# Second feed-forward matrix by Strassen's scheme, in turn with 128-feature tiles of the first matrix

## The chip, the core and the metric

The kernel runs on one core of one Trainium2 chip. A core has a matrix engine (TensorE, PE in the profile), three engines that work element by element on 128 partitions (VectorE or DVE, ScalarE or ACT, GpSimd or POOL), and SyncE (SP), which here issues the large transfers from HBM. SBUF holds the operands; PSUM, eight banks of 128 x 512 numbers, takes the products. The metric is the device time of one execution in microseconds (us), lower is better. The kernel before takes 2152.32 us (median of three runs, 2152.02 to 2153.08).

## The reference

Two hybrid attention layers run over 256 positions of 2048 features; then comes a block with block-sparse attention, a convolution and a feed-forward. Only that last part is touched:

```python
f = rms_norm(h, g_ffn_pre)                                   # 256 x 2048
f = jnp.square(jax.nn.relu(f @ w_ff1)) @ w_ff2               # 2048 -> 8192 -> 2048
h = h + rms_norm(f, g_ffn_post)
```

All data is float32. The result must be near that of float32 products.

## The kernel before

**How a float32 product is made.** The operands of PE are in fp32r, a format that keeps fewer bits. So every operand is split in two: `high`, the number rounded to fp32r, and `low`, what is left, rounded too. A product is the sum of three: high by high, high by low and low by high. Weights stream from HBM in blocks of 512 KB (128 partitions x 1024 numbers): SP loads a block into `raw` (a ring of four), ACT copies it to `high` with rounding (`round_block`, L934), DVE subtracts `high` from `raw` and writes `low` (`low_part`, L490), and PE multiplies. For 61 blocks of an earlier stage POOL makes `low` in DVE's stead, since DVE works there on the convolution (L1682, L1726, L1718).

**The feed-forward.** 256 blocks, four quarters of 64. In a quarter, eight chunks of the first matrix come first (four blocks each, 256 hidden features each). These are computed with the features on the partitions: a weight tile is the stationary operand, high and low of the normed input (`xhl`) stream past it, 512 columns at once (L682), and `low` of the weights meets the high half of the input, 256 columns (L699). A block has eight matmuls of 512 and eight of 256 columns. Then ACT and DVE add the cross term, take the square of the positive part and split it into high and low (`relu_square` L1242 to L1246, L1300, L1820). Four chunks of the second matrix follow (eight blocks each): here the hidden tile is the stationary operand and 512 columns of weights stream past it. A block holds two tiles of 128 hidden features by 512 outputs; with two halves of the positions and three partial products that makes 12 matmuls of 512 columns (L686, L687, L702). At a chunk's end DVE adds two banks of PSUM to the running sum (`ff_sum`, L1635).

**What sets the order.** All of it is written out by hand; each engine goes through its own list and waits on semaphores. `slots` interleaves a block's work with side work; PE goes through `weight_block` in the order of the plan.

Of the kernel before, what the change touches and what calls it, by code (L numbers as in the profile page):

```python
# [39 lines left out]
P = 128  # L40
S = 256
# [13 lines left out]
NQ = 4  # L55
# [39 lines left out]
def plan(a):  # L95
# [77 lines left out]
    for q in range(NQ):  # L173
        f1 = [("f1", q, j) for j in range(8)]
        if q == 0:

            run(*[chunk(k, a["w_ff1_2"][0], D * q + 256 * j, width=256, flipped=True) for j, k in enumerate(f1[:2])])
        for j, k in enumerate(f1):
            if q or j >= 2:
                flip(k, a["w_ff1_2"][0], D * q + 256 * j)  # L180
        for n, (col, width) in enumerate(FCOLS):
            add(("f2", q, n), a["w_ff2_2"][0], col, width=width, row0=D * q)
# [6 lines left out]
FF0, FF_SLOTS = BLOCK2 + BLOCK2_SLOTS, 64  # L189
# [13 lines left out]
F2_LAST = [NQ * FF_SLOTS - 8 * n + 1 for n in (3, 2, 1)]  # L203
# [26 lines left out]
def build(nc, a, out):  # L230
    by, chunk_at, acc_users = plan(a)
    with ExitStack() as ctx:
# [3 lines left out]
        def sem(name):  # L236
            return ctx.enter_context(nc.semaphore(name))

# [84 lines left out]
        rowp, rowf = cut(work, 4096, D), cut(work, 10480, D)  # L323
# [21 lines left out]
        def vec(name, n):  # L345
# [9 lines left out]
        rstd2, rstdm, rstd3, rstd4, sq3, nmr = (vec(k, 2) for k in ("rstd2", "rstdm", "rstd3", "rstd4", "sq3", "nmr"))  # L355
# [13 lines left out]
            relu_ready fsq_ready fin_ready out_done dve_done norm_dve rows_half mw_landed mw_high mw_low mw_ready csum_ready""".split()  # L369
# [7 lines left out]
         fsq_ready, fin_ready, out_done, dve_done, norm_dve, rows_half, mw_landed, mw_high, mw_low, mw_ready, csum_ready) = (sem(n) for n in names)  # L377
# [72 lines left out]
        def sums(kind, *at):  # L450

            return {"o": 0, "oa": 2 * NC, "ob": 2 * NC + 4, "f2": 3 * NC + 4}[kind] + (NF if kind == "f2" else NC) * sum(at[:-1]) + at[-1] + 1
# [35 lines left out]
        def low_part(eng, g, ready):  # L488
            eng.wait_ge(high_ready, g + 1)
            eng.tensor_tensor(part(low, g), part(raw, g), part(high, g).bitcast(F32), ALU.subtract).then_inc(ready, 1)  # L490
# [5 lines left out]
        def _(pe):  # L496
# [113 lines left out]
            def operands_ready(c, i):  # L610
# [15 lines left out]
                elif k[0] in ("o", "oa", "ob", "f2") and k[-1]:  # L626
# [7 lines left out]
                elif k[0] == "ob" and i == 0:  # L634
                    pe.wait_ge(yt_ready, 32 + H2)
                elif k[0] == "ob":
                    pe.wait_ge(ct_ready, i)
                elif k[0] == "f2":
                    pe.wait_ge(yt_ready, 40 + 8 * k[1] + i + 1)

            def weight_block(g, rows=(0, 1), between=None):
# [6 lines left out]
                vhs, vls, both = (yh, yl, yhl) if k[0] in ("mk", "mv", "o", "oa", "ob", "f2") else (xh, xl, None)  # L648
# [5 lines left out]
                tiles = [(t, c.kt0 + c.nk * i + t, s) for t in range(c.nk) for s in rows[:len(outs)]]  # L654
# [12 lines left out]
                def with_high(start, stop):  # L667
                    pe.wait_ge(high_ready, g + 1)
                    for t, kt, s in tiles:
                        if k in (("f1", 0, 0), ("f1", 0, 1)) and (t, s) == (2, rows[0]):  # L670
# [51 lines left out]
                else:  # L722
# [3 lines left out]
                    ins = with_low(g == c.blocks[-1])  # L726
                if 1 in rows:
                    ins.then_inc(block_used, 1)
                elif g == c.blocks[-1]:
# [185 lines left out]
            for b in range(NQ * FF_SLOTS):  # L915
# [4 lines left out]
                if b < NQ * FF_SLOTS - 4:  # L920
                    weight_block(FF0 + b)
            for s in range(ST):
                for b in range(NQ * FF_SLOTS - 4, NQ * FF_SLOTS):
                    weight_block(FF0 + b, (s,))
# [3 lines left out]
        def _(act):  # L928
# [18 lines left out]
            def cross_out(name):  # L947
# [4 lines left out]
                if flips.index(c):  # L952
                    act.wait_ge(folded, n)
                act.activation(cross, crosses(c), ACT.Copy).then_inc(cross_ready, 1)  # L954
# [74 lines left out]
            def squares(src, c, rows=(0, 1)):  # L1029
# [203 lines left out]
            def relu_square(name):  # L1233

                c = by[name]
# [738 lines left out]
```

## Time and profile before

| | |
|---|---|
| median of three runs | 2152.32 us |
| profiled execution: its own time (span) | 2150.6 us |
| PE busy | 2125.1 us (99%) |
| DVE busy | 1361.9 us (63%) |
| ACT busy | 1106.1 us (51%) |
| POOL busy | 156.2 us (7%) |
| DMA | 395.17 MB, mean 184 GB/s |

The profile is of one execution. Its span counts from the first to the last instruction. "Busy" of PE counts the modelled ends of its matmuls, which overlap, so that the mean duration of a matmul is longer than the distance from one to the next. The clock granted to PE is 1.00 (of 2.4 GHz) in all slices but the last few microseconds. In the two-engine view of a stretch the columns are: stretch, its length, then busy us and instruction count of PE, of its weight loads, of DVE, ACT and POOL, then PE's granted clock, the mean busy share of the 16 DMA engines and GB/s.

### The profile page before, as it was taken

To read this page: it belongs to the slowest core of one execution; us is meant where nothing else is said; L and a number is where in the kernel's file an instruction comes from. 1 tells how busy PE (TensorE), PEld (TensorE's weight loads), DVE (VectorE), ACT (ScalarE), POOL (GpSimd) and SP (SyncE) were. 2 spreads that over 40 slices of the span, in tenths; PEclk is the share of its full clock that TensorE was granted. 3 is DMA by queue.
4 is the path that set the end of the run, shared out by engine and by line. 5 is a ranking of instruction groups with operands and counts; after the bars stand their busy time and mean duration, and the time that the engine had idled before them with its cause. 6 is when DMAs were issued, how large, how long until landed. Compare 5 with 4: busy or idle time off the path is not lost. (4 is left out here: it accounts for less than half of the span.)

```text
span 2150.6 us, 29240 instructions
## 1 busy us (share of the span) xinstructions
PE 2125.1 (99%) x11602; PEld 1841.8 (86%) x11602; DVE 1361.9 (63%) x1979; ACT 1106.1 (51%) x1541; POOL 156.2 (7%) x78
## 2 busy tenths in 40 slices
PE   8999999999999999999999999999999999999998
PEld 7888888888988888888888888888888888888886
DVE  5554568875577558876578678766555555555555
ACT  4444554454464555555455455656435534544543
POOL 0000000000000000000007873000000000000000
PEclk9999999999999999999999999999999999999999
DMA  8666545655576655655656654646666666666664
GB/s 278 196 189 187 165 138 174 179 172 186 185 214 186 178 148 159 174 167 176 191 180 198 193 178 151 215 136 206 193 193 190 189 193 193 189 194 190 192 190 145
DMA packets 325031, 395.17 MB, mean 184 GB/s; under 512 B 20848, under 2 KB 252912, under 8 KB 324128
## 3 DMA queue, kind: packets, MB, share of 16 engines
q1 hardware_dynamic: 323104, 383.21, 59.0%
q0 software_dynamic: 1792, 10.10, 1.2%
q8 instruction: 92, 1.51, 0.3%
q14 instruction: 43, 0.35, 0.1%
HBM read 391.16 MB, written 2.10 MB: 183 GB/s over the span
## 5 line engine op out<-in xcount | busy, mean ns | idle before, releaser
L490 DVE TENSOR_TENSOR low<-raw,high 128x1024 fp32r<-128x1024 f32 (+2 forms) x672 | 809.9, 1209 | 639.0 <-ACT high L934 635.3
L934 ACT ACTIVATE high<-raw 128x1024 fp32r<-128x1024 f32 (+2 forms) x732 | 763.0, 1046 | 775.8 <-PE acc L682 201.7
L682 PE MATMUL acc<-xhl,high 128*128 128x512 f32 x3198 | 766.4, 391 | 0.0
L682 PEld LDWEIGHTS acc<-xhl,high 128*128 128x128 f32 x3198 | 587.0, 188 | 113.8 <-issue 0.7
L699 PE MATMUL acc<-xhl,low 128*128 128x256 f32 x3200 | 436.9, 286 | 1.9 <-DVE xhl L1792 1.4
L699 PEld LDWEIGHTS acc<-xhl,low 128*128 128x128 f32 x3200 | 414.4, 191 | 18.1 <-DVE xhl L1792 1.8
L686 PE MATMUL acc<-high,yhl 128*128 128x512 f32 (+1 forms) x1036 | 380.1, 373 | 2.2 <-DVE work L1718 1.6
L687 PE MATMUL acc<-high,yhl 128*128 128x512 f32 (+1 forms) x1036 | 378.8, 372 | 0.0
L702 PE MATMUL acc<-low,yhl 128*128 128x512 f32 (+1 forms) x1036 | 241.9, 374 | 0.2
L686 PEld LDWEIGHTS acc<-high,yhl 128*128 128x128 f32 x1036 | 195.2, 188 | 36.8 <-DVE work L1718 2.0
L687 PEld LDWEIGHTS acc<-high,yhl 128*128 128x128 f32 x1036 | 195.2, 188 | 33.8
L702 PEld LDWEIGHTS acc<-low,yhl 128*128 128x128 f32 x1036 | 182.9, 189 | 33.7 <-DVE yhl L1401 1.0
L490 POOL TENSOR_TENSOR low<-raw,high 128x1024 fp32r<-128x1024 f32 x61 | 147.9, 2437 | 81.2 <-ACT high L934 80.9
L1300 DVE TENSOR_TENSOR acc<-acc,cross 128x512 f32<-128x512 f32 x103 | 71.5, 694 | 37.2 <-ACT cross L954 37.0
L1682 DVE SCALAR_TENSOR_TENSOR tb<-work,params,tb 128x256 f32<-128x256 f32 x232 | 93.7, 480 | 0.0
L966 ACT ACTIVATE sc<-sc,small 128x128 f32<-128x128 f32 x64 | 28.6, 448 | 93.0 <-DVE small L1376 92.9
L686 PE MATMUL acc<-high,xhl 128*128 128x512 f32 (+2 forms) x224 | 73.7, 341 | 0.1
L687 PE MATMUL acc<-high,xhl 128*128 128x512 f32 (+2 forms) x224 | 73.1, 339 | 0.0
L702 PE MATMUL acc<-low,xhl 128*128 128x512 f32 (+2 forms) x320 | 72.7, 360 | 0.0
L954 ACT ACTIVATE cross<-acc 128x512 f32<-128x512 f32 x104 | 60.4, 581 | 1.9 <-PE acc L682 1.9
L702 PEld LDWEIGHTS acc<-low,xhl 128*128 128x128 f32 x320 | 53.7, 188 | 8.5 <-issue 1.3
L686 PEld LDWEIGHTS acc<-high,xhl 128*128 128x128 f32 x224 | 42.3, 189 | 5.2 <-issue 0.7
(228 smaller groups left out, 1286.9 us busy)
## 6 DMA issues: line engine op xcount, KB each, us to landing
raw<-in_w_in SPq DMA_DIRECT2D x328, 512.0 KB, 3.7
raw<-in_w_ff SPq DMA_DIRECT2D x256, 512.0 KB, 3.9
raw<-in_w_out SPq DMA_DIRECT2D x91, 512.0 KB, 4.3
raw<-in_w_mem_kv SPq DMA_DIRECT2D x32, 512.0 KB, 5.0
raw<-in_w_in SPq DMA_DIRECT2D x16, 256.0 KB, 2.7
raw<-in_w_out SPq DMA_DIRECT2D x10, 256.0 KB, 2.8
x_nat<-in_mem SPq DMA_DIRECT2D x4, 512.0 KB, 7.8
x_nat<-in_x POOLq DMA_DIRECT2D x4, 512.0 KB, 6.4
```

What stands on the lines that cost most here:

```text
L490: eng.tensor_tensor(part(low, g), part(raw, g), part(high, g).bitcast(F32), ALU.subtract).then_inc(ready, 1)
L682: ins = pe.matmul(acc[:, 2 * (c.acc % 2) + s, :], wh[:, t, at], vhl, start=first, stop=last)
L686: pe.matmul(outs[s], vh[:, at], wh[:, t, :], start=first, stop=False)
L687: ins = pe.matmul(outs[s], vl[:, at], wh[:, t, :], start=False, stop=last)
L699: ins = pe.matmul(acc[:, 2 * (c.acc % 2) + s, S:2 * S], wl[:, t, at], vh, start=crossed and t == 0, stop=last)
L702: ins = pe.matmul(outs[s], vh[:, at], wl[:, t, :], start=False, stop=last)
L934: act.activation(part(high, g), part(raw, g), ACT.Copy).then_inc(high_ready, 1)
L954: act.activation(cross, crosses(c), ACT.Copy).then_inc(cross_ready, 1)
L966: ins = act.activation(sc[:, j % 2, s, 0:n], src, ACT.Exp, bias=nmx[:, r:r + 1], accum_out=rs[:, r:r + 1])
L1300: dve.tensor_tensor(out, accs(c), cross, ALU.add).then_inc(folded, 1)
L1682: ins = dve.scalar_tensor_tensor(out=cv[:, ct, :] if tap == TAPS - 1 else sums_at, in0=src, scalar=w, in1=sums_at, op0=ALU.mult, op1=ALU.add)
```

## The change

The hidden layer has 64 tiles of 128 features. Tiles are taken in pairs; a pair by one half (1024) of the output columns is a 2 x 2 by 2 x 2 product of blocks: two position halves by two tiles, and two tiles by two column blocks of 512. Done plainly it takes eight block products. The change does 60 of the 64 such groups with seven block products (Winograd's form of Strassen's scheme), and the last four, half of the columns of pairs 28 to 31, plainly, as eight blocks (`last_block`).

- **PE** does the first 12 blocks of the first matrix as before. Then it goes in turn: `group(g)`, 21 matmuls of 512 columns (seven products, 14 with high weights, then seven with low), and `hidden_tile(g + 6)`, two blocks of one 128-feature tile of the first matrix, 16 matmuls of 512 and 16 of 256 columns. Seven banks of PSUM hold the products of four groups.
- **SP** loads a group as two transfers of 512 KB (`load_group`, into one of two buffers `bset`, when PE has finished the group two before), and the first matrix in blocks of eight row tiles by 128 columns.
- **POOL** makes, for each group, the four sums of weight blocks (`group_sums`: 512, 512 and 1024 columns), for each pair the four sums of hidden blocks (`pair_sums`: 128 columns each), and for every fourth group adds products to the running sums (`add_sums`: two of 1024).
- **ACT** rounds the seven weight blocks of a group (`split_h`: 1024, 1024, 1536 columns), the two blocks of the first matrix, the hidden tile out of PSUM (`tile_copy`) and the seven hidden blocks of a pair (`pair_h`, 896).
- **DVE** makes the low parts of all of these (`split_l`, `low_part`, `pair_l`), the squares (`hidden_rows`), and for every fourth group adds seven products out of PSUM (`sums_out`). `split_l` waits until POOL has made all sums of that group, since it writes over the weights.

The core of the diff, in the order plan, PE (`group` and its loop), DVE (`hidden_rows`, `split_l` and the loop), POOL (`group_sums` and the loop), SP:

```diff
-    for q in range(NQ):
-        f1 = [("f1", q, j) for j in range(8)]
...
-        for n, (col, width) in enumerate(FCOLS):
-            add(("f2", q, n), a["w_ff2_2"][0], col, width=width, row0=D * q)
+    for n in range(TILES_AHEAD, TILES):
+        add(("g1", n), w, P * n, width=P, nk=8)
+    for n in range(2, NF):
+        add(("f2", n), a["w_ff2_2"][0], CW * n, row0=P * (TILES - 8), kts=8)
...
+            def group(g):
...
+                pe.wait_ge(pair_ready, pair + 1)
+                hid, units = hidden(pair), bset_r[:, g % 2]
+                for n, (p, unit, combo_no) in enumerate(PRODUCTS):
+                    pe.wait_ge(split_high, 3 * g + (1, 1, 2, 2, 3, 3, 3)[n])
+                    if first:
+                        product_released(g // 4, p)
+                    for hl in range(2):
+                        pe.matmul(bank_of[p], hid[:, hl, combo_no, :], units[:, 7 + unit, :], start=first and hl == 0,
+                                  stop=False)
+                for n, (p, unit, combo_no) in enumerate(PRODUCTS):
+                    pe.wait_ge(split_low, 3 * g + (1, 1, 2, 2, 3, 3, 3)[n])
+                    ins = pe.matmul(bank_of[p], hid[:, 0, combo_no, :], units[:, unit, :], start=False, stop=last)
+                ins.then_inc(group_used, 1)
...
+            for g in range(GROUPS):
+                group(g)
+                if g + TILES_AHEAD < TILES:
+                    hidden_tile(g + TILES_AHEAD)
...
+            def hidden_rows(n):
...
+                dve.wait_ge(tile_out, n - TILES_AHEAD + 1)
+                link(dve.tensor_tensor(t[:, 0:S], t[:, 0:S], t[:, S:2 * S], ALU.add))
...
+                dve.scalar_tensor_tensor(out=combo[:, 1:3, :] if n % 2 else combo[:, 0:8:7, :], in0=v, scalar=0.0, in1=v,
+                                         op0=ALU.max, op1=ALU.mult).then_inc(relu_ready, 1)
...
+            def split_l(g, part_no):
+
+                dve.wait_ge(sum_step, 3 * g + 3)
+                dve.wait_ge(split_high, 3 * g + part_no + 1)
+                at, end = ((2, 4), (0, 2), (4, 7))[part_no]
+                dve.tensor_tensor(bset_r[:, g % 2, at:end, :], bset[:, g % 2, at:end, :], bset_r[:, g % 2, 7 + at:7 + end, :].bitcast(F32),
+                                  ALU.subtract).then_inc(split_low, 1)
...
+            for g in range(GROUPS):
+                n, ahead = g + TILES_AHEAD - 1, g + 1 < GROUPS
+                if g and n < TILES:
+                    hidden_rows(n)
+                if g:
+                    low_block(FF1 + 2 * g)
+                    low_block(FF1 + 2 * g + 1)
+                if ahead:
+                    split_l(g + 1, 0)
+                    split_l(g + 1, 1)
+                if g % 4 == 3:
+                    sums_out(g // 4)
+                if ahead:
+                    split_l(g + 1, 2)
+                if g % 2 == 0 and n < TILES:
+                    pair_l(g // 2 + 2)
...
+            def group_sums(g):
+
+                units = bset[:, g % 2]
+                pool.wait_ge(group_landed[g % 2][0], 16 * (g // 2 + 1))
+                pool.tensor_tensor(units[:, 1, :], units[:, 1, :], units[:, 0, :], ALU.subtract).then_inc(sum_step, 1)
...
+                pool.tensor_tensor(units[:, 4, :], units[:, 3, :], units[:, 1, :], ALU.subtract).then_inc(sum_step, 1)
+                pool.wait_ge(sum_step, 3 * g + 2)
+                t2 = units[:, 4, :].unsqueeze(1).broadcast_to([P, 2, CW])
+                pool.tensor_tensor(units[:, 5:7, :], t2, units[:, 0:3:2, :], ALU.subtract).then_inc(sum_step, 1)
...
+            for g in range(GROUPS):
+                if g + 1 < GROUPS:
+                    group_sums(g + 1)
+                if g % 2 == 0 and g + TILES_AHEAD - 1 < TILES:
+                    pair_sums(g // 2 + 2)
+                if g % 4 == 0 and g:
+                    add_sums(g // 4 - 1)
...
+            def load_group(g):
...
+                    sp.wait_ge(group_used, g - 1)
```

What this does to DVE's list, before: in the feed-forward, between two chunks of the first matrix. `low` and `raw` are the weight block, `yhl` the hidden rows, `acc` and `cross` are in PSUM and SBUF.

```order
L1300 TENSOR_TENSOR acc<-acc,cross 128x2x256
L490 TENSOR_TENSOR low<-raw,high 128x1024 x2
L1820 TENSOR_TENSOR yhl<-cb,yhl 128x512
L490 TENSOR_TENSOR low<-raw,high 128x1024 x2
L1300 TENSOR_TENSOR acc<-acc,cross 128x2x256
```

In its place stands, on DVE, for an even step (`bset`, `bset_r` are the weight blocks of a group, `combo` and `hid` the hidden blocks of a pair, `raw_r` the low block):

```order
L2014 TENSOR_TENSOR tile_b<-tile_b 128x256
L2017 SCALAR_TENSOR_TENSOR combo<-tile_b 128x256
L518 TENSOR_TENSOR raw_r<-raw,high 128x1024 x2
L2034 TENSOR_TENSOR bset_r<-bset,bset_r 128x1024 x2
L2034 TENSOR_TENSOR bset_r<-bset,bset_r 128x1536
L2027 TENSOR_TENSOR hid<-combo,hid 128x896
```

and for every fourth step, with the products `sbank`, `tb` and `acc` in PSUM, the running sums `msum`, and `au` and `u` between them:

```order
L2014 TENSOR_TENSOR cross<-cross 128x256
L2017 SCALAR_TENSOR_TENSOR combo<-cross 128x2x128
L518 TENSOR_TENSOR raw_r<-raw,high 128x1024 x2
L2034 TENSOR_TENSOR bset_r<-bset,bset_r 128x1024 x2
L2051 TENSOR_TENSOR msum<-msum,sbank 128x512
L2052 TENSOR_TENSOR msum<-msum,tb 128x512
L2053 TENSOR_TENSOR msum<-msum,acc 128x512
L2055 TENSOR_TENSOR msum<-msum,acc 128x512
L2059 TENSOR_TENSOR au<-au,acc 128x512
L2061 TENSOR_TENSOR u<-au,acc 128x512
L2062 TENSOR_TENSOR msum<-msum,acc 128x512
L2034 TENSOR_TENSOR bset_r<-bset,bset_r 128x1536
```

A step on DVE is thus two low blocks of the first matrix and seven low blocks of 512 for the group, where before it was one instruction of 1024 columns for each 512 KB.

POOL's list before, to its end (`L490` are the 61 low blocks of the earlier stage; the two last transfers load gain vectors):

```order
L1907 DMA yf<-in_ln_gain 128x2048
L1908 DMA yf<-in_ln_bias 128x2048
L490 ISA
L490 TENSOR_TENSOR low<-raw,high 128x1024 x61
L1913 DMA work<-in_g_mix_post 128x2048
L1916 DMA work<-in_g_ffn_post 128x2048
L232 UNCONDITIONAL_BRANCH
```

POOL's list now, from the middle of the feed-forward; in all there are 60 such triples on `bset`, 32 such quadruples on `combo` and 15 pairs on `msum`:

```order
L2242 TENSOR_TENSOR combo<-combo 128x128
L2243 TENSOR_TENSOR combo<-combo 128x128
L2245 TENSOR_TENSOR combo<-combo 128x128
L2247 TENSOR_TENSOR combo<-combo 128x128
L2253 TENSOR_TENSOR msum<-msum,au 128x1024
L2256 TENSOR_TENSOR msum<-msum,u 128x1024
L2230 TENSOR_TENSOR bset<-bset 128x512
L2233 TENSOR_TENSOR bset<-bset 128x512
L2236 TENSOR_TENSOR bset<-bset 128x1024
```

What POOL had after its last low block was only the two transfers; now it has three instructions for each group, between DVE's own.

## Rows read from the trace of the kernel before

**Rows 1.** The page: span, then busy time of each engine.

```profile
span 2150.6 us, 29240 instructions
PE 2125.1 (99%) x11602; PEld 1841.8 (86%) x11602; DVE 1361.9 (63%) x1979; ACT 1106.1 (51%) x1541; POOL 156.2 (7%) x78
```

**Rows 2.** Stretches of the feed-forward and of the end, busy us and granted clock.

```profile
1610.00:2100.00 490.00, 490.00 (x2521) 420.70 (x2520) 261.34 (x248) 241.79 (x278) 0.00 (x0) 1.00 0.62 191
2145.00:2151.00 6.00, 0.00 (x0) 0.00 (x0) 2.71 (x4) 0.00 (x0) 0.00 (x0) 0.68 0.49 175
```

**Rows 3.** Groups by shape inside 1610:2100: busy us, mean ns, then idle before.

```profile
L490 DVE TENSOR_TENSOR low<-raw,high 128x1024 fp32r<-128x1024 f32 x179 | 219.4, 1226 | 230.2 <-ACT high L934 230.2
L934 ACT ACTIVATE high<-raw 128x1024 fp32r<-128x1024 f32 x178 | 188.7, 1060 | 246.9 <-PE acc L699 71.8 <-PE acc L702 67.0 <-PE acc L687 61.1
L954 ACT ACTIVATE cross<-acc 128x512 f32<-128x512 f32 x24 | 13.9, 579 | 0.0
L1635 DVE SCALAR_TENSOR_TENSOR work<-acc,small,work 128x512 f32<-128x512 f32 x20 | 14.0, 745 | 0.0
L1820 DVE TENSOR_TENSOR yhl<-cb,yhl 128x512 fp32r<-128x512 f32 x24 | 16.4, 685 | 0.0
```

**Rows 4.** Timeline of PE (start us, us): first-matrix blocks, then second-matrix blocks.

```profile
1491.09 3.82 PE L682 MATMUL acc<-xhl,high 128*128 128x512 f32 x16
1496.66 3.82 PE L682 MATMUL acc<-xhl,high 128*128 128x512 f32 x16
...
2105.42 1.98 PE L702 MATMUL acc<-low,yhl 128*128 128x512 f32 x8
2110.86 1.52 PE L702 MATMUL acc<-low,yhl 128*128 128x512 f32 x6
```

**Rows 5.** Timeline of PE where twelve feed-forward blocks are done.

```profile
1468.82 3.82 PE L682 MATMUL acc<-xhl,high 128*128 128x512 f32 x16
```

**Rows 6.** Timeline of POOL, four of its 61 instructions beside busy DVE.

```profile
1141.73 2.99 POOL L490 TENSOR_TENSOR low<-raw,high 128x1024 fp32r<-128x1024 f32 x1 [52.79 <-ACT high L934]
...
1147.49 2.40 POOL L490 TENSOR_TENSOR low<-raw,high 128x1024 fp32r<-128x1024 f32 x1
1149.85 2.60 POOL L490 TENSOR_TENSOR low<-raw,high 128x1024 fp32r<-128x1024 f32 x1
...
1315.62 2.40 POOL L490 TENSOR_TENSOR low<-raw,high 128x1024 fp32r<-128x1024 f32 x1 [2.83 <-ACT high L934]
```

**Rows 7.** Timeline of DVE over the same time.

```profile
1140.10 2.36 DVE L490 TENSOR_TENSOR low<-raw,high 128x1024 fp32r<-128x1024 f32 x2
...
1144.01 1.26 DVE L1718 TENSOR_TENSOR work<-work,cb 128x512 f32<-128x512 f32 x1
...
1148.22 1.95 DVE L1726 SCALAR_TENSOR_TENSOR work<-work,params,cb 128x256 f32<-128x256 f32 x1 [2.35 <-ACT cb L1192]
1150.10 2.64 DVE L1726 SCALAR_TENSOR_TENSOR work<-work,params,cb 128x256 f32<-128x256 f32 x1
...
1316.93 2.17 DVE L490 TENSOR_TENSOR low<-raw,high 128x1024 fp32r<-128x1024 f32 x1 [0.17 <-ACT high L934]
```

**Rows 8.** Groups by shape: POOL in 1240:1310, DVE in 1141:1316.

```profile
L490 POOL TENSOR_TENSOR low<-raw,high 128x1024 fp32r<-128x1024 f32 x23 | 54.8, 2399 | 15.0 <-ACT high L934 14.8
...
L1682 DVE SCALAR_TENSOR_TENSOR tb<-work,params,tb 128x256 f32<-128x256 f32 x217 | 87.4, 480 | 0.0
```

**Rows 9.** Timeline of PE, its last instruction.

```profile
2141.46 0.39 PE L687 MATMUL acc<-high,yhl 128*128 128x512 f32 x1
```

**Rows 10.** DMA issues in 1420:2110, KB each, median us to landing.

```profile
raw<-in_w_ff SPq DMA_DIRECT2D x249, 512.0 KB, 3.9
```

More of the change, by code:

```diff
@@ L653, in weight_block @@
                 wh, wl = part(high, g), part(low, g)
-                tiles = [(t, c.kt0 + c.nk * i + t, s) for t in range(c.nk) for s in rows[:len(outs)]]
+                tiles = [(t, c.kt0 + c.nk * i + t, s) for t in range(c.nk) for s in range(2)]
                 crossed = k == ("f1", 0, 0) and i == 0
@@ new lines, in product_released @@
+            def product_released(k, p):
+                if k == 0:
+                    if p in (5, 6, 7, 4):
+                        pe.wait_ge(relu_ready, 2 if p in (5, 6) else 3)
+                elif p == 1:
+                    pe.wait_ge(first_out, k)
+                else:
+                    pe.wait_ge(out_step, 7 * (k - 1) + OUT_STEP[p])
+            def group(g):
+                pair, _ = where(g)
+                first, last = pair % 4 == 0, pair % 4 == 3
+                pe.wait_ge(pair_ready, pair + 1)
[11 more added lines that the diff above has]
+                ins.then_inc(group_used, 1)
@@ new lines, in first_copy @@
+            def first_copy(k):
+                act.wait_ge(group_used, 4 * k + 4)
+                if k:
+                    act.wait_ge(out_added, 2 * k - 1)
+                act.activation(au[:, 0, :], bank_of[1], ACT.Copy).then_inc(first_out, 1)
+            cross_out(("f1", 0, 0))
+            round_block(FF0 + 10)
+            round_block(FF0 + 11)
+            cross_out(("f1", 0, 1))
+            pair_h(0)
+            round_block(FF1)
+            for part_no in range(3):
+                split_h(0, part_no)
@@ new lines, in _ @@
+            n_sq = 16 + 2 * NC
+            for g in range(BLOCKS - 4, BLOCKS - 1):
+                low_block(g)
+            dve.wait_ge(rowf_landed, 16)
+            gain_sums(0, n_sq + 2)
+            low_block(BLOCKS - 1)
+            gain_sums(1, n_sq + 4)
+            dve.wait_ge(block_used, by["f2", 2].blocks[-1] + 1)
+            for s in range(ST):
+                ins = dve.tensor_tensor(m_cols(2)[:, s, :], m_cols(2)[:, s, :], last_banks[2][s], ALU.add)
+            ins.then_inc(sum_ready, 1)
@@ L1834, in _ @@
+            dve.wait_ge(sum_ready, sums("f2", 2))
+            gain_sums(2, n_sq + 6)
+            for s in range(ST):
+                rows, at = m_cols(3)[:, s, :], slice(s, s + 1)
                 if s:
-                    acc_done(last)
+                    dve.wait_ge(block_used, BLOCKS)
                 else:
                     dve.wait_ge(rows_half, 1)
-                dve.scalar_tensor_tensor(out=rows, in0=accs(last)[:, s, :], scalar=sq3[:, at], in1=rows, op0=ALU.mult,
-                                         op1=ALU.add).then_inc(sum_ready, 1)
```

425 lines of the change are left out of this document (314 added, 111 removed).

## The prediction

> **What bounds the kernel now.** I read the page's busy times first. The reader is to see that PE is busy for 99% of a span of 2150.6 us, that DVE and ACT have 37 and 49% to spare, and that POOL is nearly idle [rows 1]. Then the stretch view of the middle of the feed-forward: PE is busy for all 490 of 490 us at the full clock, DVE for 261 us and ACT for 242 [rows 2]. The groups of that stretch say who waits for whom there: DVE sits idle before its low blocks until ACT has rounded, and ACT sits idle until PE frees a buffer [rows 3]. So PE alone sets the pace, and matmuls taken from it come off the end, as long as no other engine becomes slower than PE. The timelines give the pace. Two blocks of the first matrix take 1496.66 - 1491.09 = 5.57 us, 2.785 each, and two of the second 2110.86 - 2105.42 = 5.44 us, 2.72 each or 0.2267 us for each of its 12 matmuls of 512 columns [rows 4].
>
> **PE after the change.** The second matrix costs 128 x 2.72 = 348.2 us now. After, 60 groups of 21 matmuls are 60 x 4.76 = 285.6 us and eight plain blocks 21.8 us, together 307.4: 40.8 us less. The first matrix keeps its columns, 12 blocks and then 58 tiles of two blocks, 5.57 us each. One step (a group and a tile) is 10.33 us of PE. That is what the other engines must keep up with.
>
> **DVE and POOL by themselves.** DVE's instruction of 1024 columns takes 1.23 us, one of 512 takes 0.685 [rows 3]: 0.54 us for 512 columns and 0.14 fixed. Each step it has two low blocks (2.45), three splits of 1024, 1024 and 1536 (1.23 + 1.23 + 1.77 = 4.23), two of 256 columns for the squares (0.83), half of a pair's 896 columns (0.55), and a quarter of seven instructions of 512 out of PSUM, between 0.685 and 0.745 each [rows 3], 1.2. Sum 9.3 us: it fits in 10.33. POOL's instruction of 1024 columns takes 2.40 us where nothing disturbs it [rows 8]. Each step it has 2048 columns of group sums, half of 512 for a pair, a quarter of 2048 for the running sums: 2816 columns, 6.6 us. That fits too. ACT: 3584 columns of splits, two blocks, a tile, half a pair, by 1.06 us for 1024 and 0.58 for 512 [rows 3], is about 7.1 us. It fits.
>
> **DVE and POOL together.** They do not run beside each other. The only place where the trace shows both at once is the stretch in which POOL makes low blocks, and there the ends of the instructions tell it [rows 6, 7]:
> - POOL's block of 1315.62 ends at 1318.02. DVE's block, begun at 1316.93, ends at 1319.10, 1.08 us after POOL's end, though it takes 1.23 us alone: it did next to nothing while POOL ran.
> - POOL's block of 1141.73 ends at 1144.72; DVE's 512 columns of 1144.01 end 0.55 us later.
> - POOL's block of 1147.49 ends at 1149.89; DVE's 256 columns of 1148.22 end 0.28 us later. POOL's next ends at 1152.45; DVE's next ends again 0.29 us later, at 1152.74, after 2.64 us.
> - The other way round, POOL's block of 1141.73 begins while DVE's pair from 1140.10 runs to 1142.46, and takes 2.99 us in place of 2.40.
>
> All these DVE instructions read two operands in SBUF. L1682, which reads one in SBUF and one in PSUM, runs 217 times beside POOL at 480 ns [rows 8] and shows nothing of it. The Trainium skill (SBUF — State Buffer, section Who interferes with whom) says the same in general: a VectorE instruction with two SBUF inputs and a GpSimd instruction that reads SBUF share a port by an exclusive lock, and the second one blocks until the first is done. If it were a split of bandwidth instead, the block of 1316.93 would have got half of its columns done in the 1.09 us of overlap and ended near 1318.7; the trace has 1319.10.
>
> In the changed kernel nearly all of DVE's work (splits, low blocks, squares, pairs; all but the sums out of PSUM) reads twice from SBUF, and all of POOL's sums read SBUF. So their times add up. For a step:
> - DVE holds the port for 1.08 us for 1024 columns (above). 2048 + 3584 + 512 + 448 = 6592 columns: 6.95 us.
> - POOL holds it for the distance between two ends less DVE's part, 2.56 - 0.28 = 2.28 us for 1024 [rows 6, 7]. 2816 columns: 6.27 us.
> - The sums out of PSUM are 1.05 us in which DVE does nothing else; POOL could run beside them, but seldom has work just then. Changes of turn and short waits on DVE's own results: 0.1.
>
> The sum is 14.4 us for a step, against PE's 10.33. Its bounds: 13.2 if the sums out of PSUM lie wholly beside POOL, and 9.3 + 6.6 = 15.9 if whole durations add, fixed parts too. I take 14.4, since the rows show blocked instructions without their fixed part. For POOL's sums of 128 columns there is no row; by proportion 0.3 us each, with a fixed part like DVE's 0.44, which is 0.3 us a step at most and inside the bounds.
>
> Nothing else is later. The loop through the transfer: a group's buffer comes free at PE's end of a group, two transfers land 4 to 6 us later (3.9 us for one of 512 KB now, [rows 10]; the rows of the first matrix get half as long, which I put at up to 1 us), POOL's three sums with DVE's turns between them take 4.6 + 3.5, ACT has rounded meanwhile, DVE's three splits with POOL's turns 7, PE's last products 0.7. That is some 22 us for two steps of 28.8. On SP, what queues behind a `load_group` are the two blocks for two steps later.
>
> **The sum.** Twelve blocks are done at 1468.82 + 1.83 = 1470.6 us, half way through the 16 matmuls of that row [rows 5]. I add 5 us of waiting for the first group (POOL's first sums, ACT's and DVE's first splits in a line; 0 to 12), 4.8 for group 0, and 12 for the step in which DVE's list is shorter. Then 58 steps of 14.4 are 835.2. At the end 2 us for the release of the banks, 21.8 for the eight plain blocks, and from PE's last matmul to the end 2150.6 - 2141.85 = 8.8 us as now [rows 1, 9]. 1470.6 + 5 + 4.8 + 12 + 835.2 + 2 + 21.8 + 8.8 = 2360. The median of the runs is 1.7 us above the profiled span, so 2362 us. With 13.2 a step it is 70 less, 2292; with 15.9 it is 87 more, 2449.
>
> **Rivals.**
> - *The change works as counted: PE stays the bound.* DVE's and POOL's own sums, 9.3 and 6.6 us, are both below 10.33, so this is what busy times alone would say. 1470.6 + 5 + 4.8 + 59 x 4.76 + 58 x 5.57 + 21.8 + 8.8 = 2115, and 1.7: 2117 us, 1.6% faster. It needs POOL's plain f32 sums to leave DVE alone, where its f32 to fp32r low blocks do not. It decides at 10.33 us: DVE's 9.3 leave 1.0 us for all of POOL's 6.3. The five overlaps above speak against it. Chance 10%.
> - *The port is shared by turns, but POOL is faster at plain f32 than at its low blocks.* No row shows POOL with f32 output. If it were as fast as DVE, 1.23 us for 1024, its part would be 3.4 us, a step 11.4, the whole 2362 - 58 x 3.0 = 2188 us, still slower. Anything between lies between. Chance 9%.
> - *More than the sum.* PE waits some 4 us in each step. It has no such gap in the middle of the kernel now; after its last matmul the granted clock of 2145:2151 is 0.68, a mean of the full level and of half [rows 2]. If the clock fell to 1.2 GHz in each gap and a third of a step's matmuls ran at half speed, a step would cost PE 10.33 x 1.33 = 13.8 us, which still fits in 14.4. With half of them it is 15.5, 1.1 us more than the port's 14.4, and the whole 2362 + 58 x 1.1 = 2426 us; with all of them 20.7 us and over 2700. It decides at four tenths of the matmuls. The Trainium skill (TensorE: Matmul & The Clock Gate, section Why this matters for your kernels) warns of this fall after idle gaps; that the gap is long enough here, no row shows. Chance 7%.
>
> **Chances and range.** The forecast of adding up (2292 to 2449) has 74%. Faster by over 0.2% (which is about what a measurement of this kernel can tell from no change) comes only with the first rival: 10%. Within 0.2%: 1%, a step of 10.8 us by chance. Slower: 89%. The range 2240 to 2440 leaves out the first rival, the lower half of the second, and the top of the third and of the sum.
>
> **What would show it.** In the profile after: PE busy well under 99%, with some 70% in the stretch from 1500 us on, and its idle time ended by DVE's splits (L2034). POOL busy some 400 us more. The mean of DVE's 1024-column splits and low blocks at 1.8 to 2.5 us in place of 1.23, while its sums out of PSUM stay at 0.69. The distance between two groups on PE 14.4 us. I am wrong if the DVE durations stay at 1.23 beside POOL; then the end is near 2117. If PE's idle time is ended by DMA or by ACT, the loop through the transfer was the bound and my margin of 7 us there was wrong. If the granted clock falls in the stretch, the third rival is at work.

## The result, and the profile after

The changed kernel takes 2356.5 us (median of four, 2354.2 to 2357.8) against 2152.7 for the kernel before: a ratio of 1.0945, 95% interval 1.093 to 1.0961. Its profiled execution has a span of 2356.0 us. The forecast was 2362.

The page after, which answers to [rows 1]: span, busy times, and of the 40 slices those of PE, DVE, POOL and PE's clock.

```profile
span 2356.0 us, 29862 instructions
PE 2176.2 (92%) x11422; PEld 1856.9 (79%) x11422; DVE 1844.8 (78%) x2205; ACT 1170.1 (50%) x1584; POOL 839.1 (36%) x417
...
PE   8999999999999999999999999788888888888886
...
DVE  5555578665765687757867867899999999999996
...
POOL 0000000000000000000587202687878787878882
PEclk9999999999999999999999999898989898988898
```

The last 15 slices are the changed part. DVE goes from mostly 5 tenths to 9, POOL from 0 to 8, and PE, at 9 there before, falls to 8. The stretch view of its middle (columns as in [rows 2]) and the waits of PE there (who waited for whom, us in all, times, longest):

```profile
1600.00:2100.00 500.00, 421.23 (x1878) 344.16 (x1878) 498.48 (x329) 227.12 (x241) 400.69 (x195) 0.89 0.50 150
...
PE obank L804 <- DVE raw_r L518: 62.7, 30, 4.5
PE sbank L836 <- DVE hid L2027: 12.9, 5, 2.7
```

DVE is busy for 498 of 500 us and no longer waits for anyone; PE is busy for 421 at a mean clock of 0.89 and waits for DVE. In the groups by shape of that stretch, DVE and then POOL, the mean of one instruction is what to look at, beside [rows 3, 8]:

```profile
L2034 DVE TENSOR_TENSOR bset_r<-bset,bset_r 128x1024 fp32r<-128x1024 f32 x72 | 122.3, 1737 | 0.0
L518 DVE TENSOR_TENSOR raw_r<-raw,high 128x1024 fp32r<-128x1024 f32 x70 | 116.0, 1697 | 0.0
L2034 DVE TENSOR_TENSOR bset_r<-bset,bset_r 128x1536 fp32r<-128x1536 f32 x36 | 88.6, 2461 | 0.0
L2027 DVE TENSOR_TENSOR hid<-combo,hid 128x896 fp32r<-128x896 f32 x18 | 49.1, 2727 | 0.0
L2014 DVE TENSOR_TENSOR cross<-cross 128x256 f32<-128x256 f32 x18 | 37.1, 2059 | 0.0
...
L2061 DVE TENSOR_TENSOR u<-au,acc 128x512 f32<-128x512 f32 x9 | 6.2, 687 | 0.3
...
L2236 POOL TENSOR_TENSOR bset<-bset 128x1024 f32<-128x1024 f32 x35 | 104.5, 2987 | 2.7
L2230 POOL TENSOR_TENSOR bset<-bset 128x512 f32<-128x512 f32 x36 | 70.5, 1959 | 47.3 <-DMA bset<-in_w_ff 47.3
L2245 POOL TENSOR_TENSOR combo<-combo 128x128 f32<-128x128 f32 x18 | 25.9, 1439 | 0.0
```

A block of 1024 columns takes DVE 1.70 to 1.74 us, where it took 1.23; the 256 columns on `cross` take 2.06, five times the 0.42 that they take with nobody in the way; the sums out of PSUM keep their 0.69 us. POOL's 1024 columns take 2.99 us, where a block of 1024 took 2.40, and its 128 columns 1.44; waits for the other engine count in all of these. Both are longer beside each other, and DVE only where it reads twice from SBUF. The timelines of DVE and then POOL show the turns:

```profile
1810.89 2.29 DVE L2034 TENSOR_TENSOR bset_r<-bset,bset_r 128x1024 fp32r<-128x1024 f32 x1
1813.11 2.31 DVE L2034 TENSOR_TENSOR bset_r<-bset,bset_r 128x1024 fp32r<-128x1024 f32 x1
1815.34 0.68 DVE L2051 TENSOR_TENSOR msum<-msum,sbank 128x512 f32<-128x512 f32 x1
...
1819.64 1.75 DVE L2034 TENSOR_TENSOR bset_r<-bset,bset_r 128x1536 fp32r<-128x1536 f32 x1
...
1810.44 1.66 POOL L2230 TENSOR_TENSOR bset<-bset 128x512 f32<-128x512 f32 x1 [2.03 <-DMA bset<-in_w_ff]
1812.25 2.09 POOL L2233 TENSOR_TENSOR bset<-bset 128x512 f32<-128x512 f32 x1
1814.41 3.25 POOL L2236 TENSOR_TENSOR bset<-bset 128x1024 f32<-128x1024 f32 x1
```

POOL's first sum ends at 1812.10 and DVE's block at 1813.18, 1.08 us later. POOL's second ends at 1814.34 and DVE's second block at 1815.42, 1.08 us later again, as in [rows 6, 7]. POOL's third, of 1024 columns, begins at 1814.41 and takes 3.25 us: it waits for the rest of DVE's block and then runs beside the sums out of PSUM, which pay nothing for it. The split of 1819.64, with POOL idle, takes 1.75 us.

### The profile page after: what moved, and what is told of

Its sections match the earlier page's. It is cut to its first block and busy times, and to the rows that moved or that the text cites. A ratio compares the mean times of both kernels' runs of the same rounds, so it can differ in the third digit from the quotient of the medians.

```text
span 2356.0 us, 29862 instructions
## 1 busy us (share of the span) xinstructions
PE 2176.2 (92%) x11422; PEld 1856.9 (79%) x11422; DVE 1844.8 (78%) x2205; ACT 1170.1 (50%) x1584; POOL 839.1 (36%) x417
## 5 line engine op out<-in xcount | busy, mean ns | idle before, releaser
L518 DVE TENSOR_TENSOR low<-raw,high 128x1024 fp32r<-128x1024 f32 (+2 forms) x428 | 512.0, 1202 | 337.0 <-ACT high L1099 333.4
L740 PE MATMUL acc<-xhl,high 128*128 128x512 f32 x2270 | 544.6, 391 | 0.0
L740 PEld LDWEIGHTS acc<-xhl,high 128*128 128x128 f32 x2270 | 416.5, 188 | 80.8 <-issue 0.7
L2034 DVE TENSOR_TENSOR bset_r<-bset,bset_r 128x1024 fp32r<-128x1024 f32 x180 | 341.9, 1945 | 0.0
L1413 ACT ACTIVATE bset_r<-bset 128x1024 fp32r<-128x1024 f32 x180 | 210.1, 1194 | 138.1 <-POOL bset L2230 71.4
L797 PE MATMUL obank<-xhl,high 128*128 128x512 f32 x928 | 246.2, 410 | 0.0
L797 PEld LDWEIGHTS obank<-xhl,high 128*128 128x128 f32 x928 | 182.5, 202 | 36.7
L518 DVE TENSOR_TENSOR raw_r<-raw,high 128x1024 fp32r<-128x1024 f32 x124 | 201.8, 1665 | 7.4 <-ACT high L1099 7.4
L744 PE MATMUL acc<-high,yhl 128*128 128x512 f32 (+1 forms) x524 | 180.9, 358 | 2.2 <-DVE work L1913 1.6
L745 PE MATMUL acc<-high,yhl 128*128 128x512 f32 (+1 forms) x524 | 179.7, 356 | 0.0
L518 POOL TENSOR_TENSOR low<-raw,high 128x1024 fp32r<-128x1024 f32 x61 | 147.9, 2436 | 81.2 <-ACT high L1099 80.9
L2236 POOL TENSOR_TENSOR bset<-bset 128x1024 f32<-128x1024 f32 x60 | 174.3, 2906 | 4.7
L836 PE MATMUL acc<-bset_r,hid 128*128 128x512 f32 x480 | 131.0, 414 | 12.1 <-DVE combo L2007 11.7
```

The source lines that it names most:

```text
L518: eng.tensor_tensor(out, part(raw, g), part(high, g).bitcast(F32), ALU.subtract).then_inc(ready, 1)
L740: ins = pe.matmul(acc[:, 2 * (c.acc % 2) + s, :], wh[:, t, at], vhl, start=first, stop=last)
L744: pe.matmul(outs[s], vh[:, at], wh[:, t, :], start=first, stop=False)
L745: ins = pe.matmul(outs[s], vl[:, at], wh[:, t, :], start=False, stop=last)
L797: ins = pe.matmul(obank[:, :], wh[:, t, :], flat(xhl[:, 8 * i + t]), start=i == 0 and t == 0, stop=i == 1 and t == 7)
L836: pe.matmul(bank_of[p], hid[:, hl, combo_no, :], units[:, 7 + unit, :], start=first and hl == 0, stop=False)
```

## The experiments

Theory: DVE's instructions with two operands in SBUF and POOL's sums exclude each other, so that their times add up to a step above PE's 10.33 us. All kernels below are the changed one with the edit shown, cut to its core. "Step" is the mean distance between the ends of two groups on PE, over the 58 from the second group to the last; it is 14.06 us in the changed kernel. A kernel of which only the span is given was executed once; the others have the median of four executions and their profiled span.

**One memset for each sum.**

```diff
+            def fill(out, done):
+
+                pool.memset(out, 0.5).then_inc(done, 1)
+
...
-                pool.tensor_tensor(units[:, 1, :], units[:, 1, :], units[:, 0, :], ALU.subtract).then_inc(sum_step, 1)
+                fill(units[:, 1, :], sum_step)
```
(and so for all nine sums.)

> The changed kernel with each of GpSimd's sums replaced by one memset of the same output (the sums of weight blocks, of hidden blocks and of products are left out; every wait and every transfer stays). Theory (DVE and POOL add up, because both read SBUF through one port): DVE's blocks of 1024 columns are back at 1.23 us, its step is 9.3 us, PE's 10.33 us sets the pace; span 2356 - 58 x (14.06 - 10.33) = 2140 us, within 15. Rival A (the loop through the transfers with rows of 512 bytes, or ACT, sets the step): the time stays above 2300 us, since neither is touched.

Span 2131.3 us, step 10.34. A stretch of it, and DVE's two groups of 1024 columns:

```profile
1600.00:1900.00 300.00, 300.00 (x1543) 257.50 (x1543) 251.80 (x272) 185.62 (x197) 82.95 (x163) 1.00 0.68 204
...
L2034 DVE TENSOR_TENSOR bset_r<-bset,bset_r 128x1024 fp32r<-128x1024 f32 x58 | 68.3, 1218 | 0.0
L518 DVE TENSOR_TENSOR raw_r<-raw,high 128x1024 fp32r<-128x1024 f32 x58 | 68.3, 1218 | 0.0
```

PE is busy all the time at the full clock, and DVE is back at 1.22 us. The transfers, the rows of 512 bytes and ACT are as in the changed kernel, so rival A is out: POOL's sums alone made the 225 us. It came out 9 us under the expected 2140, since the start is shorter too (group 0 ends at 1483.4 in place of 1491.6). DVE's own list is 251.8 / 300 x 10.34 = 8.7 us a step.

**Three memsets for each sum.**

```diff
+            def fill(out, done):
+
+                for value in (0.5, 0.25):
+                    pool.memset(out, value).then_inc(filled, 1)
+                    n_filled[0] += 1
+                    pool.wait_ge(filled, n_filled[0])
+                pool.memset(out, 0.125).then_inc(done, 1)
...
-                pool.tensor_tensor(units[:, 1, :], units[:, 1, :], units[:, 0, :], ALU.subtract).then_inc(sum_step, 1)
+                fill(units[:, 1, :], sum_step)
```
(and so for all nine sums.)

> As the run with one memset, but each sum is three memsets of its output one behind the other (the sums are left out again), so that GpSimd is busy about as long as with the sums (3 x 0.86 us for 1024 columns, by the 3.52 us of the 4096-column memset after the change) but never reads SBUF. Theory in its narrow form (only reads collide): DVE stays at 1.23 us for 1024 columns, span near 2140 us. Rival B (any GpSimd instruction on SBUF blocks DVE's two-operand instructions for its length): 6.95 + 7.1 + 1.05 = 15.1 us a step, span above 2400 us.

Span 2162.3 us, step 10.73.

```profile
1600.00:1900.00 300.00, 294.22 (x1490) 247.25 (x1490) 241.82 (x260) 181.02 (x189) 239.75 (x466) 1.00 0.66 197
...
L2034 DVE TENSOR_TENSOR bset_r<-bset,bset_r 128x1024 fp32r<-128x1024 f32 x57 | 67.3, 1220 | 55.7 <-POOL bset L2234 55.7
```

POOL is busy for 240 of 300 us, as much as with the sums, and DVE's instructions stay at 1.22 us. So it is not POOL's activity that blocks DVE, nor its writing, but its reading: rival B is out. The Trainium skill (SBUF — State Buffer, section Who interferes with whom) draws the same line, between a GpSimd instruction that reads SBUF and one that only writes; the 1.22 us agree. The 22 us over 2140 are a wait of another kind: DVE waits for POOL to finish, 55.7 us in the row. The chain from landing through POOL to the splits is a little too long for PE's pace.

**Copies for sums.**

```diff
-                pool.tensor_tensor(units[:, 4, :], units[:, 3, :], units[:, 1, :], ALU.subtract).then_inc(sum_step, 1)
+                pool.tensor_copy(units[:, 4, :], units[:, 3, :]).then_inc(sum_step, 1)
```
(all nine in this manner.)

> As the changed kernel, but each of GpSimd's sums is a copy of one of its two operands (the adding is left out). It reads once from SBUF where the sum reads twice. Theory (a GpSimd instruction that reads SBUF at all holds the port for its length): DVE's blocks are longer than 1.23 us, and the step is 6.95 + the copies' time + about 0.8; no row has the copies' length, if it is half of the sums' (3.1 us a step) the step is 10.9 us and the span 2175 us, if it is the same, 2356. Rival C (only two-operand instructions on both sides collide): DVE at 1.23 us, 2140 us.

Span 2151.4 us, step 10.65, under the 2175 expected of copies half as long as sums. Groups of DVE, then POOL:

```profile
L518 DVE TENSOR_TENSOR raw_r<-raw,high 128x1024 fp32r<-128x1024 f32 x58 | 81.6, 1446 | 0.0
L2014 DVE TENSOR_TENSOR cross<-cross 128x256 f32<-128x256 f32 x14 | 14.6, 1042 | 0.0
...
L2235 POOL COPY bset<-bset 128x1024 f32<-128x1024 f32 x28 | 39.4, 1408 | 1.7
```

DVE's blocks are longer (1.45 us for those of the tile, 1.27 for the splits, and 256 columns 1.04), so one read is enough to collide and rival C is out. But a copy of 1024 weight columns takes POOL 1.41 us, waits included, against 2.99 for a sum, and that nearly lets PE keep its pace.

**All sums on DVE.**

```diff
             for g in range(GROUPS):
                 n, ahead = g + TILES_AHEAD - 1, g + 1 < GROUPS
+                if ahead:
+                    group_sums(g + 1)
                 if g and n < TILES:
                     hidden_rows(n)
+                if g % 2 == 0 and n < TILES:
+                    pair_sums(g // 2 + 2)
...
                     sums_out(g // 4)
+                    add_sums(g // 4)
```
(the three functions move from POOL's list to DVE's, with `dve` for `pool`.)

> All of GpSimd's sums moved into DVE's list; GpSimd has nothing left there but a memset and a transfer. Theory (adding up): DVE's step is 9.3 us + 2.6 (sums of weight blocks, 0.69 + 0.69 + 1.23) + 0.6 (half of four of 128 columns) + 0.6 (a quarter of two of 1024) = 13.1 less 0.08 for each of 12 instructions that follow without a pause, 12.2 to 13.1 us; span 2356 - 58 x (1.0 to 1.9) = 2246 to 2300 us: faster than the changed kernel though DVE has more to do, still slower than before. Rival D (DVE's 14.06 us a step are its own work and GpSimd's comes free beside it): 14.06 + 3.8 us a step, 2575 us.

2255.2 us, ratio 1.0476 (1.0459 to 1.0493) to before; span 2253.2, step 12.40. DVE's blocks take 1.22 us and its own sum of 1024 columns 1.23:

```profile
L2034 DVE TENSOR_TENSOR bset_r<-bset,bset_r 128x1024 fp32r<-128x1024 f32 x48 | 56.5, 1217 | 0.0
...
L2080 DVE TENSOR_TENSOR bset<-bset 128x1024 f32<-128x1024 f32 x25 | 30.6, 1225 | 0.8
```

DVE has 3.7 us more to do in each step, and the kernel is 101 us faster. POOL's help costs DVE 14.06 - 8.7 = 5.4 us a step, doing the work itself 3.7. Rival D is out.

**Only the weight sums on DVE** (`group_sums` in DVE's list as above, the two others left with POOL).

> Only the sums of weight blocks go to DVE; GpSimd keeps those of hidden blocks and of products. Adding up, with the parts as the runs so far have them: DVE's own list, one behind the other, 8.7 us a step (the one-memset run: busy 251.8 of 300 us at 10.34 a step), plus 2.45 for the weight sums on DVE, plus what GpSimd still holds, 768 columns or 1.7 us, of which some lies beside the sums out of PSUM: 12.2 to 12.9 us a step. Span 2253 + 58 x (-0.2 to 0.5) = 2241 to 2282 us, about the time of the run with all sums on DVE. Rival H (small GpSimd loads are free, only long ones collide): 11.2 us a step, 2185 us.

2282.9 us, ratio 1.0603 (1.0587 to 1.0619); span 2279.8, step 12.86: inside the range at its upper end, 28 us slower than with all sums on DVE. POOL still has two sums of 128 columns and half of one of 1024 in a step, 1.7 us by the forecast's price, and 12.86 - 8.7 - 2.45 = 1.7 us is what it costs. Two thirds of these columns are in long sums, which would make 0.5 x 2.28 = 1.1 us alone. That the short ones cost too is seen on DVE's pair of low blocks, first with POOL idle, then beside the short sums that begin at 1839.59:

```profile
1825.45 2.35 DVE L518 TENSOR_TENSOR raw_r<-raw,high 128x1024 fp32r<-128x1024 f32 x2
1839.42 2.61 DVE L518 TENSOR_TENSOR raw_r<-raw,high 128x1024 fp32r<-128x1024 f32 x2
```

One short sum ends in that time and the pair is 0.26 us longer; two of them a step are the missing 0.5 to 0.6 us (an estimate). Rival H is out.

**Fewer products on PE.**

```diff
-                                  stop=False)
-                for n, (p, unit, combo_no) in enumerate(PRODUCTS):
-                    pe.wait_ge(split_low, 3 * g + (1, 1, 2, 2, 3, 3, 3)[n])
-                    ins = pe.matmul(bank_of[p], hid[:, 0, combo_no, :], units[:, unit, :], start=False, stop=last)
+                                  stop=last and hl == 1 and n < 6)
+                pe.wait_ge(split_low, 3 * g + 3)
+                p, unit, combo_no = PRODUCTS[-1]
+                ins = pe.matmul(bank_of[p], hid[:, 0, combo_no, :], units[:, unit, :], start=False, stop=last)
```

> The changed kernel without six of the seven low products of each group (left out: the low parts of six weight blocks in the product; their rounding and subtracting on ACT and DVE stay). PE's step falls by 6 x 0.227 = 1.36 us to 8.97. Theory (DVE and GpSimd by turns at the port set the step): span within 12 us of 2356. Rival E (PE, or PE at half clock behind its gaps, is part of the step): 58 x 1.36 = 79 us less, 2277.

Span 2360.9 us (2356.0 expected, rival 2277), step 14.2. Taking 79 us of matmuls away gains nothing: PE's work is not in the step. The clock falls further, 0.85 in the stretch:

```profile
1600.00:2100.00 500.00, 383.44 (x1646) 308.11 (x1645) 498.52 (x323) 225.40 (x238) 397.04 (x193) 0.85 0.47 147
```

**More products on PE.**

```diff
                     else:
+                        with_high(True)
                         with_high()
                         ins = with_low()
```
(`with_high(True)` makes the eight matmuls of a block's high half and leaves the bank open.)

> The changed kernel with eight more matmuls of 512 columns in each tile of the first matrix: the high products of its first block are made twice, the second time over the first. PE's step is 10.33 + 1.83 = 12.16 us, and its gaps are shorter, so the granted clock should fall less. Theory: 12.16 is under 14.06 and DVE is never idle, so the span stays within 15 us of 2356. Rival F (the falls of the clock cost time in the changed kernel): faster by 20 us and more, with a clock nearer to 1. Rival E (PE's work is in the step): 58 x 1.83 = 106 us more.

> The kernel with the eight repeated matmuls once more, now timed in rounds: the one look had 2340.2 us, 15.8 under the changed kernel's span, at a clock of 0.98 for 0.96. If the falls of PE's clock cost some 0.25 us a step, the median stays 12 to 20 us under 2356.5. If it was chance, it is within 5 us of it.

The first of the two expectations is answered by one execution, with a span of 2340.2 us. The second is answered by four: 2343.2 us, ratio 1.0886 (1.0868 to 1.0904), which is 13.3 us under the changed kernel's median; step 13.78.

```profile
1600.00:2100.00 500.00, 465.85 (x2222) 387.70 (x2221) 497.92 (x336) 235.06 (x247) 401.05 (x201) 0.96 0.51 153
```

More work on PE makes the kernel faster by 0.6%, which is clear of the noise: at the edge of what my theory allowed (15 us) and short of rival F (20 us and more). The clock is 0.96 in the stretch where it was 0.89, but it is not shown that the clock gives the time back. DVE is as full as before, 497.9 of 500 us, so it gets through its list 0.28 us a step sooner, and the traces show where. These are the stretches in which DVE adds the products out of PSUM, two in a row of them, in the changed kernel and then here; POOL's busy time is the fifth of the five:

```profile
1815.34:1819.73 4.39, 3.60 (x13) 1.86 (x12) 4.36 (x9) 4.27 (x5) 2.32 (x1) 1.00 0.40 120
1869.00:1873.39 4.39, 4.39 (x28) 3.96 (x27) 4.36 (x9) 1.75 (x3) 1.29 (x1) 1.00 0.98 310
```

```profile
1808.52:1812.91 4.39, 4.39 (x22) 3.60 (x20) 4.36 (x9) 2.32 (x3) 4.17 (x3) 1.00 0.58 161
1863.05:1867.43 4.38, 4.38 (x29) 3.93 (x28) 4.34 (x9) 0.30 (x1) 3.23 (x3) 1.00 0.66 220
```

The two stretches recur every eight steps. POOL works beside them for 3.6 us in the changed kernel and for 7.4 here, 0.45 and 0.92 us a step; in the run with fewer products, whose step is longer, it is 3.0 us (0.00 and 3.02). There POOL costs DVE nothing. POOL's first sum of a group waits for the transfer, and the transfer for PE to free the buffer: it begins 4.9 us before the first stretch in the changed kernel (1810.44) and 1.1 us before it here (1807.45). So a PE with more to do seems to put POOL's sums off into the place where they are free. That this alone makes the 13.3 us, no run isolates; a part for the clock stays open.

**Eight plain products in the same order.**

```diff
-PRODUCTS = ((2, 2, 1), (3, 3, 6), (1, 0, 0), (5, 1, 3), (6, 4, 4), (7, 5, 5), (4, 6, 2))
+PRODUCTS = ((2, 2, 1), (3, 3, 1), (1, 2, 2), (5, 3, 2), (2, 0, 0), (3, 1, 0), (1, 0, 3), (5, 1, 3))
...
-                act.activation(hidden(pair)[:, 0], combo[:, 0:7, :], ACT.Copy).then_inc(pair_high, 1)
+                act.activation(hidden(pair)[:, 0, 0:4], combo[:, 0:4, :], ACT.Copy).then_inc(pair_high, 1)
```
(no sums; four banks.)

> The order of the changed kernel (each group in turn with a tile of the first matrix in rows of 512 bytes, the group's weights in rows of 4 KB) with eight plain products for seven: four banks, 24 matmuls a group, and no sums of weights or of hidden blocks at all. PE's step is 5.57 + 5.44 = 11.01 us, DVE's about 6.8. Theory: PE is the bound again; 58 steps of 11.01, and less waiting for the first banks at the start: 2165 us, within 10. Rival A (order and rows cost in themselves): the step stays above 11.5 us, over 2200.

2161.7 us, ratio 1.0041 (1.0026 to 1.0056); span 2159.3, step 10.94.

```profile
1600.00:2100.00 500.00, 500.00 (x2544) 428.08 (x2544) 285.11 (x343) 218.23 (x254) 0.00 (x0) 1.00 0.64 192
```

The order itself keeps PE busy all the time, with DVE at 57%, and rival A is out here too. What it costs against before, 8.7 us of span, is mostly at the end: from the last group to the end of the span it takes 38.0 us, as in the changed kernel (37.9), where eight plain blocks and the old end would be 21.8 + 8.8 = 30.6. Against the run with one memset it also shows what seven products for eight are worth on PE when nothing else is in the way: 2159.3 - 2131.3 = 28 us, 36 by the steps alone, of which the longer start of that run takes 8.

**Another order at the start.**

```diff
+            pair_h(1)
+            cross_out(("f1", 0, 2))
             for c in range(4):
                 x_squares(c)
-            pair_h(1)
-            cross_out(("f1", 0, 2))
```
(and on DVE likewise.)

> The changed kernel with one piece of the lists of ACT and DVE in another order at the start: the third chunk's cross term and squares come ahead of the eight sums of squares of x. PE waits 11.7 us there for the squares of that chunk (they free two banks). Expected: that wait goes to 2 us or less, span 2346 us, within 4. Rival G (DVE is the bound from the first step on, so that a wait of PE moved away comes back as a later one): under 3 us gained.

2354.5 us, ratio 1.0934 (1.0916 to 1.0952), not to be told from the changed kernel's 1.0945. PE's wait there, in the changed kernel and then with the edit:

```profile
1486.57 2.05 PE L836 MATMUL acc<-bset_r,hid 128*128 128x512 f32 x4 [11.72 <-DVE combo L2007]
```

```profile
1484.15 2.04 PE L836 MATMUL acc<-bset_r,hid 128*128 128x512 f32 x4 [10.37 <-DVE combo L2007]
```

My reason was wrong, and rival G near the truth: the wait is 1.3 us shorter, not 9.7, the span 3.0. The third chunk's squares stand in DVE's list behind the splits of the first group and a pair, and those run beside POOL's sums. That DVE's lateness there is what PE waits for fits the run with one memset, where group 0 ends 8 us sooner; it is not taken apart further.

**The shortest list for DVE that I found** (all sums on DVE; in addition):

```diff
-                            ins = pe.matmul(obank[:, :], wh[:, t, :], flat(xhl[:, 8 * i + t]), start=i == 0 and t == 0,
+                            pe.matmul(obank[:, 0:S], wh[:, t, :], xh[:, 8 * i + t, :], start=i == 0 and t == 0, stop=False)
+                            ins = pe.matmul(obank[:, 0:S], wh[:, t, :], xl[:, 8 * i + t, :], start=False,
                                             stop=i == 1 and t == 7)
...
-                act.activation(tile_buf[n % 2], obank[:, :], ACT.Copy).then_inc(tile_out, 1)
+                act.activation(tile_buf[n % 2][:, 0:S], obank[:, 0:S], ACT.Relu).then_inc(tile_out, 1)
...
+                act.activation(combo[:, 1:3, :] if n % 2 else combo[:, 0:8:7, :], v, ACT.Square).then_inc(relu_ready, 1)
```

> The run with all sums on DVE, with DVE's list made as short as I can: PE adds the low product of a tile of the first matrix into the same 256 columns (three matmuls of 256 for one of 512 and one of 256; 0.15 us more a step), ACT takes the positive part and the square out of PSUM in two instructions of 256, so DVE's two of 256 columns are gone (0.7 us a step), and the order at the start is the one of the start run. DVE is the bound at 12.4 - 0.7 = 11.7 us a step: span 2253 - 58 x 0.7 = 2212 us, within 12; slower than before (2151) still, since a step would have to be under 10.7 us. Rival I (ACT's added wait for DVE's pairs makes a new stall): no gain on 2253.

2210.4 us, ratio 1.027 (1.0255 to 1.0285); span 2207.8, step 11.63 (11.7 expected), so rival I is out. It is the best with seven products, 146 us under the changed kernel and 57 over the kernel before. No version here that makes the whole result beats the kernel before.

## Why the prediction was right

The mechanism was the forecast one at each link that an experiment touches: PE's own step of 10.33 us (10.34 with memsets), DVE's list under it (8.7), the port shared by turns, the sum of both above PE. That the span came within 4 us, in a range of 200, is luck in part: the errors of the terms are up to 20 us and cancel. The terms of the sum, as forecast and as measured:

| term | forecast | measured |
|---|---|---|
| end of group 0 | 1470.6 + 5 + 4.8 = 1480.4 | 1491.6 |
| first step | 12 | 10.9 |
| 58 steps | 14.4 each, 835.2 | 14.06 each, 815.6 |
| last group to the end | 2 + 21.8 + 8.8 = 32.6 | 37.9 |
| span | 2360 | 2356.0 |

So the 4 us of error are +11.2 - 1.1 - 19.6 + 5.3.

- **The step, 0.34 us too long.** I had written that POOL would seldom have work beside the sums out of PSUM. It has, for 0.45 us a step (the two stretches shown with the repeated matmuls): POOL's third sum is put off by DVE's blocks until those sums begin. Less that, the forecast's sum is 13.9 us; the 0.1 us that is left is not taken apart. The lower bound of 13.2 asked for all of the 1.05 us to lie there.
- **DVE's own list, 8.7 us and not 9.3.** I had added whole durations; instructions that follow each other at once overlap (two of 1.22 us take 2.35). POOL adds 14.06 - 8.7 = 5.4 us, less than the 6.27 for which it holds the port by the forecast. Of the other 0.9, 0.45 lie beside the sums out of PSUM. The rest may be fixed parts of blocks that POOL held up (1.08 us after POOL's end, for 1.22 alone); that is argued and not measured.
- **POOL's 128 columns.** One with nobody in its way takes 0.46 us, 0.02 above what I had allowed (0.3 to 0.44); in the stretch it shows 1.44, the rest being its wait for DVE.

```profile
1467.44 0.46 POOL L2243 TENSOR_TENSOR combo<-combo 128x128 f32<-128x128 f32 x1
```

- **Who ends PE's waits.** I named the splits, L2034. It is L518, the low blocks of the tile, in 30 waits of up to 4.5 us. DVE's list is one row, so where PE catches up with it depends on the order, and here it does so in the tile. The steps are not alike either: eight in a row are 10.3, 11.8, 18.9, 10.3, 16.5, 10.3, 19.7 and 14.8 us, and so again. PE goes at its own pace until it has used up what lies ready, then waits. A step of 14.4 was right as a mean and wrong as a picture.
- **Signs that came otherwise.** DVE's blocks are at 1.70 to 1.74 us in the mean, under the 1.8 to 2.5 forecast. PE is busy for 84% of the stretch where I had some 70%: its matmuls take longer while the clock is down. POOL is busy for 683 us more, where I had 400: its waits for DVE count as busy.
- **The start, 11 us short.** I had 5 us of waiting, 0 to 12 as its range; PE waited 11.7 us for two banks. I had counted the line to the first split and not the release of the banks that the third chunk still held. Besides, PE came to group 0 at 1471.9, 1.3 us later than put, and made the part of the group behind the wait at half the clock (0.50 in the row), so that its matmuls took 8.0 us and not 4.8:

```profile
1486.57:1491.60 5.03, 5.03 (x12) 4.01 (x13) 4.32 (x3) 0.05 (x1) 4.95 (x4) 0.50 0.02 5
```

- **The end, 5 us short.** Two waits of PE, 1.0 us for the release and 2.1 for a low block, and 12.3 us in place of 8.8 from PE's last matmul to the end; the plain blocks themselves took 0.7 us more than put. Why the last stretch is longer is not taken apart; it is 12.3 us in the run with plain products too.
- **The third rival was partly there.** The clock did fall in PE's gaps, to a mean of 0.57 in this one:

```profile
1836.00:1848.00 12.00, 7.88 (x26) 6.74 (x27) 12.00 (x6) 4.71 (x5) 11.55 (x6) 0.57 0.28 91
```

With the step's matmuls at 0.89 of the clock PE needs some 10.33 / 0.89 = 11.6 us (an estimate) and still fits in 14.06, as the rival's own sum had it. That nothing is gained with fewer matmuls says the same. The run with repeated matmuls, in which the clock came back to 0.96, gained 13 us in all, and POOL's sums moved there as well, so how much of that is the clock's stays open.
- **Faster rivals.** POOL's sums in plain f32 are as slow as its low blocks (2.39 us for 1024 columns at the end of the kernel, where DVE is idle), so the second rival's condition does not hold. The first rival's time, 2117 us, is what the run with memsets shows but for start and end (2131).

## What to carry to other kernels

A busy share is no measure of free time where two engines share a port: add up the instructions that read two operands from SBUF on DVE and all that read SBUF on POOL, and compare the sum with the bound, before work is given to POOL. When the sum was too large here, work done on DVE itself was cheaper than POOL's help (3.7 us a step against 5.4), and only POOL work that fell beside DVE's reads of PSUM, or that only wrote, was free. Where POOL's sums fall in DVE's list matters too: twice as much of them beside the reads of PSUM went with a step 0.28 us shorter. Strassen's scheme saves one product in eight on the matrix engine, 36 us of steps here, and asks for 5632 columns of sums and splits of weights per group where the plain form needs 2048.

## What the runs showed of the hardware

- POOL's memsets, 240 us in 300, do not touch DVE's two-operand instructions (1.22 us for 1024 columns); its copies, one read, do (1.27 to 1.45 us); its sums do (1.70 to 1.74).
- DVE's instructions of 512 columns with one operand in PSUM are free of it: 0.68 to 0.69 us beside POOL and without.
- A POOL sum of 128 columns takes 0.46 us alone, shows 1.44 beside a full DVE, and makes DVE's pair of blocks 0.26 us longer.
- A block of 1024 columns that POOL held back ends 1.08 us after POOL's end in all three cases read, before and after the change.
- PE's granted clock is at the lower of its two levels (0.50, 1.2 GHz) for the five microseconds after a wait of 11.7 us, and 0.57 in the mean of 12 us that begin in a wait of 4.3 us and hold another of 1.2. Over 500 us with waits of up to 4.5 us it is 0.89, with eight more matmuls a step 0.96.
